# A two-layer kernel from its even output on: both token tiles through each step, or tile by tile with the row gathers of the tile ahead in between

## What is computed

```python
# l = 0: even mixer (convolution and pooling)       -> x   "e_out"
#        x = x + cross_attention(rmsnorm(x), mem)   -> "x_..."
#        x = x + peer_ffn(rmsnorm(x), ...)          -> "p_..."
# l = 1: x = x + sparse_attn_hgrn_mixer(rmsnorm(x)) -> "o_...", "h_...", the odd mixer
#        x = x + cross_attention(...)
#        x = x + peer_ffn(...)
# out = rmsnorm(x)

def peer_ffn(h, wq, sub_keys, u, v):              # per block of 128 tokens
    q = (xb @ wq).reshape(PEER_BLOCK, 8, 2, 128)
    s = jnp.einsum('thpd,hpnd->thpn', q, sub_keys)
    s1, i1 = lax.top_k(s[:, :, 0], 16)
    s2, i2 = lax.top_k(s[:, :, 1], 16)
    ...                                           # 16 x 16 sums, the best 16 of them per head
    g = jax.nn.softmax(top, axis=-1)              # 8 x 16 = 128 experts of 16384 for each token
    act = jax.nn.gelu(jnp.einsum('td,ted->te', xb, u[eid]))
    return jnp.einsum('te,ted->td', g * act, v[eid])
```

## Time and profile before

| | us |
|---|---|
| median of 3 runs | 2677.15 |
| profiled execution | 2676.58 |
| its span, first to last instruction | 2674.3 |
| last addition of the even output | 731 |
| gathers of layer 0, first issue | 885 |
| odd mixer, cross attention, queries of layer 1 | about 1580 to 2005 |
| last gather issued | 2641 |

### The profile page before, as it was taken

How to read it: one execution, slowest core, us unless ns; L and a number is a source line. 1 busy time by engine, 2 the same in 40 slices (tenths; PEclk the granted TensorE clock), 3 DMA queues, 4 the chain that set the end, 5 groups by cost and what they waited for, 6 DMA issues and landing times. The chain is left out here.

```text
span 2674.3 us, 23831 instructions
## 1 busy us (share of the span) xinstructions
PE 2111.0 (79%) x8566; PEld 1373.4 (51%) x8566; DVE 1453.6 (54%) x3135; ACT 653.1 (24%) x1247; POOL 1141.1 (43%) x809
## 2 busy tenths in 40 slices
PE   3899989999688498887778768858775887878776
PEld 3755679888577344333333337847672333333332
DVE  6353232147535977755555545672388776455554
ACT  1322333443233111111111124233331111111111
POOL 2612457797536333332333338214362333333332
PEclk7898989999898799999999989979898989989988
DMA  8455445565324599999999956113337999999996
GB/s 318 144 174 166 168 145 171 167 193 176 118 94 144 229 424 425 422 419 389 393 426 426 426 223 194 62 52 114 102 136 320 426 425 426 421 379 426 426 423 291
DMA packets 126934, 735.58 MB, mean 275 GB/s; under 512 B 14264, under 2 KB 14264, under 8 KB 60512
## 3 DMA queue, kind: packets, MB, share of 16 engines
q0 software_dynamic: 77600, 555.18, 49.9%
q1 hardware_dynamic: 49072, 178.83, 20.5%
q10 hardware_dynamic: 144, 0.05, 0.0%
HBM read 732.94 MB, written 1.06 MB: 274 GB/s over the span
## 5 line engine op out<-in xcount | busy, mean ns | idle before, releaser
L579 POOL TENSOR_TENSOR W_lo<-W,W_hi 128x1024 fp32r<-128x1024 f32 x264 | 642.6, 2442 | 423.7 <-ACT W_hi L1136 423.0
L800 PE MATMUL banks<-arena 128*128 128x512 f32 x912 | 449.5, 642 | 150.4 <-ACT arena L1191 150.4
L800 PE MATMUL banks<-rows_b,arena 128*128 128x512 f32 x684 | 341.1, 646 | 122.0 <-ACT arena L1191 122.0
L1136 ACT ACTIVATE W_hi<-W 128x1024 fp32r<-128x1024 f32 x264 | 277.4, 1058 | 471.3 <-PE banks L714 389.0
L800 PEld LDWEIGHTS banks<-arena 128*128 128x128 f32 x912 | 182.0, 204 | 405.3 <-issue 259.2
L2027 DVE SCALAR_TENSOR_TENSOR arena<-arena,banks 128x1024 f32<-128x1024 f32 x228 | 276.3, 1220 | 193.3 <-DMA arena<-in_uv,p_eid 192.1
L636 POOL DMA_INDIRECT arena<-in_uv,p_eid x228 | 214.8, 942 | 385.0 <-PE banks L800 376.4
L714 PE MATMUL banks<-HT_hi,W_hi 128*128 128x256 f32 x1128 | 327.2, 290 | 35.2 <-DVE HT_lo L1576 13.4
L714 PE MATMUL banks<-HT_hi,W_lo 128*128 128x256 f32 x1128 | 324.8, 288 | 0.0
L714 PE MATMUL banks<-HT_lo,W_hi 128*128 128x256 f32 x1128 | 324.6, 288 | 0.0
L800 PEld LDWEIGHTS banks<-rows_b,arena 128*128 128x128 f32 x684 | 138.7, 208 | 317.7 <-issue 206.9
(11 more groups left out here) (260 smaller groups left out, 2641.4 us busy)
## 6 DMA issues: line engine op xcount, KB each, us to landing
W<-in_weights SPq DMA_DIRECT2D x336, 512.0 KB, 3.6
gain<-in_rows POOLq DMA_DIRECT2D x10, 512.0 KB, 5.9
arena<-in_uv,p_eid POOLq DMA_INDIRECT x228
rows_b<-in_uv,p_eid POOLq DMA_INDIRECT x171
arena<-in_rows POOLq DMA_DIRECT2D x1, 2048.0 KB, 17.0
arena<-in_keys POOLq DMA_DIRECT2D x2, 1024.0 KB, 5.0
arena<-bias_scratch POOLq DMA_DIRECT2D x2, 1024.0 KB, 7.7
rows_c<-in_uv,p_eid POOLq DMA_INDIRECT x113, 10.9
```

The source lines that it names most:

```text
L579: po.tensor_tensor(W_lo[:, slot, :], W[:, (PARTS * n + part) % RAW_RING, :], W_hi[:, slot, :].bitcast(F32), ALU.subtract).then_inc(S_("lo_ ...
L800: mm = pe.matmul(sums[c], diag[:, n % DIAGS, :], rows[slot][:, D + c * BLK:D + (c + 1) * BLK], start=j == 0, stop=j == SEL - 1)
L1136: act.activation(W_hi[:, q % SPLIT_RING, :], wait_landed(act, n, part), ACT.Copy).then_inc(S_("hi_made"), 1)
```

## The change

The code up to the even output stays. From there on the work is cut into four chains, `CHAINS` = (layer 0, tile 0), (0, 1), (1, 0), (1, 1). Chain c does odd (layer 1), cross and query work of one token tile, and between its steps each engine has places (`feed`) at which it takes one group of rows of chain c-1. What is left of the groups after the chain runs at its end (`drain`); the rows of chain 3 come alone. In detail:

- Rows are taken in groups of two (64 groups a tile) instead of four, through a ring of eight slots instead of nine.
- At a feed DVE makes two dots and three small operations (L2098 to L2104 of the new file), ScalarE a tanh, two Identity with scale and bias, and two diagonals, PE the weighing of the group before. Gelu is written out with tanh.
- H of the gathers is read by DVE from SBUF; the two `p_h` banks go.
- Products are native fp32 (`dense`), tile by tile: 128 tokens moving under stationary weights, or 512 columns under stationary tokens, with a feed after each half of a weight tile. `high`, `low` and the splits of the activations go. Every weight tile of this part is read for both token tiles: 56 tiles instead of 30, counting those for the memory.
- GpSimd has only the gathers in its queue; keys, masks, gains and the bias table are loaded by SP in between the weights (`tables`), with waits of their own.
- Most copies out of PSUM move from DVE to ScalarE.
- The output is written tile by tile.

```diff
-RING = 9
-GROUP = 4
+RING = 8
+GROUP = 2
+CHAINS = [(l, t) for l in range(2) for t in range(2)]
...
+            def weigh(g):
+                c = at[0]
+                for j in range(g * GROUP, (g + 1) * GROUP):
+                    n, slot, turn = row_of(c, j)
+                    pe.wait_ge(S_("diag_ready"), n + 1)
+                    for b in range(2):
+                        mm = pe.matmul(banks[:, plan.bank(f"p_v{c}", b), :], diag[:, n % DIAGS, :],
+                                       rows[slot][:, D + b * BLK:D + (b + 1) * BLK], start=j == 0, stop=j == SEL - 1)
                     mm.then_inc(rows_done, 1)
...
+            def feed():
+                if at[0] is not None:
+                    if 1 <= at[1] <= GROUPS:
+                        weigh(at[1] - 1)
+                    at[1] += 1
...
+            def dense(stage, i, blocks):
+                n = tile_no[stage] + i
+                bank = claim(stage, i)
+                for part in range(PARTS):
+                    w = raw(n, part)
+                    for b, (out, columns, stationary) in enumerate(blocks):
+                        for j in range(2):
+                            x, y = w[:, j, columns], HT[:, 2 * part + j, :]
+                            mm = pe.matmul(bank[:, out], x if stationary else y, y if stationary else x,
+                                           start=part + b + j == 0,
+                                           stop=part == PARTS - 1 and b == len(blocks) - 1 and j == 1)
+                    mm.then_inc(pe_filled if part == PARTS - 1 else S_("part_used"), 1)
+                    if part % 2:
+                        feed()
...
+            def row_weights(g):
+                c = at[0]
+                e = slice(g * GROUP, (g + 1) * GROUP)
+                act.wait_ge(S_("dots_ready"), c * GROUPS + g + 1)
+                step(act.activation(p_tanh[:, e], p_poly[:, e], ACT.Tanh, scale=0.7978845608028654))
                 for j in range(g * GROUP, (g + 1) * GROUP):
+                    step(act.activation(p_w[:, j:j + 1], p_tanh[:, j:j + 1], ACT.Identity, scale=p_half[:, j:j + 1],
+                                        bias=p_half[:, j:j + 1]))
...
+                for n in range(PH // 2):
+                    feed()
+                    take(p_qT[l], f"p_q{n}.{c}")
+                    feed()
+                    if n:
+                        act.wait_ge(S_("lists_ready"), (PH // 2) * c + n)
+                    take(p_s[l], f"p_s{n}.{c}")
...
+                for n in range(PH // 2):
+                    after(v, f"p_s{n}.{c}")
+                    top_lists(l, n)
+                    if n < PH // 2 - 1:
+                        feed()
+                    candidates(l, 2 * n, 2 * n + 2)
+                    top_heads(l, 2 * n, 2 * n + 2)
+                    keys_of(l, t, 2 * n, 2 * n + 2)
+                    if n < PH // 2 - 1:
+                        feed()
+                if c == 1:
+                    feed(16)
...
             for c, (l, t) in enumerate(CHAINS):
+                if c:
+                    begin(c - 1)
+                if l:
+                    odd(c, t)
+                cross(c, l, t)
+                queries(c, l, t)
+                if c == 1:
+                    memory()
+                if c:
+                    drain()
+            begin(3)
+            drain()
```

More of the change, by code:

```diff
@@ L197, in make_plan @@
     p.add("e_out", 4)
[L198 to L246, removed]
+    for c, (l, t) in enumerate(CHAINS):
+        chain(p, c, l, t)
+        if c:
+            p.release(f"p_v{c - 1}")
+        p.add(f"p_v{c}", 2, marks=0, hold=True)
+    p.release("p_v3")
     return p
@@ L1017, in odd @@
-                for u in range(8):
-                    t, p = u // 4, u % 4
-                    bank = claim("idx", u)
+                after(pe, f"o_hq.{c}")
+                bank = claim(f"h_diag.{c}")
+                for hd in range(HH):
+                    mm = pe.matmul(bank[:, hd * P:(hd + 1) * P], h_kT[:, hd, :], h_qT[:, hd, :], start=True, stop=True)
+                mm.then_inc(pe_filled, 1)
+                dense(f"o_iq.{c}", 0, blocks4)
+                pe.wait_ge(S_("hscores_ready"), c - 1)
@@ L1194, in _, with take_turned, squares @@
+            def take_turned(stage):
+                for i in range(2):
+                    take(HT[:, 4 * i:4 * i + 4, :], stage, i)
+            def squares(t):
+                step(act.activation(H[:, t, :], X[:, t, :], ACT.Square, accum_out=stat(604, 1)), "squares_ready")
             act.dma_start(cols[:], io["cols"]).then_inc(S_("cols_in"), 16)
@@ L1399, in _ @@
[L1399 to L1400 removed]
+                step.free(act.activation(h_f, filled(act, f"o_hf.{c}"), ACT.Sigmoid), f"o_hf.{c}")
+                feed(2)
+                take(h_i[:, t, :], f"o_hi.{c}")
+                feed()
+                take(o_cT[:, t * P:(t + 1) * P], f"o_cT.{c}", cut=slice(0, P))
+                feed()
+                step(act.activation(h_g, filled(act, f"o_hg.{c}"), ACT.Sigmoid), "hg_sigmoid")
@@ new lines, in feed, with drain @@
+            def feed(n=1):
+                for _ in range(n):
+                    if at[0] is not None and at[1] < GROUPS:
+                        dots(at[1])
+                        at[1] += 1
+            def drain():
+                c = at[0]
+                l, t = CHAINS[c]
+                for g in range(at[1], GROUPS):
+                    dots(g)
+                at[0] = None
+                v.wait_ge(rows_done, (c + 1) * SEL)
+                for b in range(2):
+                    xs = X[:, t, b * BLK:(b + 1) * BLK]
+                    step.free(v.tensor_tensor(xs, banks[:, plan.bank(f"p_v{c}", b), :], xs, ALU.add), f"p_v{c}", b)
```

1244 lines of the change are left out of this document (702 added, 542 removed).

## The result

The changed kernel takes **2555.4 us** (median of 4 runs, 2553.9 to 2559.3), the one before 2680.7 in the same series. The ratio is **0.9535**, 95% interval 0.9511 to 0.9558. The forecast said 2627 us, 1.9% less than before; the gain is 125 us where 50 were forecast. Because the kernel before moved a little from series to series (medians of 2680.7 to 2686.6 us), small differences between two changed kernels are given by medians and, where it matters, by the two ratios to before as well. The profiled execution has a span of 2557.4 us.

What follows compares the result with a forecast made beforehand. Gathers were taken as DMA-bound, the work between them not, so the change overlaps the two. 731 + 150 + 448 + 483 + 495 + 318 = 2625 us of span, predicted as 2627; 8-in-10 range 2450 to 2760.

Steps and rivals of the forecast that it cites:

- What bounds the kernel, and which stretches would change: Row gathers are bound by DMA, the 154 + 425 us between them are not; everything to 731 us stays.
- the price of a list pass: Query work: one DVE pass of four score blocks and two heads takes 17.6 us, the first 21.3.
- Half a tile with a group, 7.2: Weight products with row weighing: PE takes (3.4 + 3.4)/0.95 = 7.2 us at a granted clock of 0.95.
- A level: Odd work, chains 2 and 3: four DVE operations of 0.69 and a group, 5.9 us each, 47 for eight.
- the odd parts' 28: Odd work of chains 2 and 3, forecast at 538 us together and measured at 510.
- That TensorE sets the dense slot: Half tiles with a group: PE sets the 7.2 us, although DMA needs 7.4, as parts and rows are there beforehand.
- The ring: Eight row slots turn in 19.7 us; the median landing of 10.9 fits, the worst, 16.1, would add 90.
- ScalarE's 2.1 us: Query list passes: DVE waits three times 2.1 us a chain while ScalarE copies scores behind the group's 1.4.
- The last rows: Chain 3's rows alone: 6 for the norm, 60 groups x 4.92 = 295, and 17 from last landing, 318 us.
- elastic: Rival, chance 0.18: rings and prefetch smooth the slots, each stage costs only its largest total, DMA; 2381 us.
- Low clock: Rival, chance 0.17: waits between PE's pieces lower the clock to 0.72, PE-bound slots cost 9.5; +193, 2820 us.
- Serial slots: Rival, chance 0.13: in 63 slots without weight tile engines wait for each other, 9.3 instead of 5.3; +252, 2879.

Runs made afterwards that it cites:

- half the products: Changed kernel leaving out every second product of the weight tiles in chains 1 to 3, loads unchanged: 2540.5 us, ratio 0.9455.
- half the bytes: Changed kernel leaving out half the bytes of each weight part in chains 1 to 3, products unchanged: 2541.6 us, ratio 0.9476.
- the experiment: Changed kernel with six row slots instead of eight, nothing else: 2675.1 us, ratio 0.9948.

## Right and wrong, by the prediction's steps

- **What bounds the kernel, and which stretches would change**: right. DMA share 9 lies in the dense parts, stages came in the forecast order, gathers began at 817 (forecast 826) and ended at 2528 (2590).
- **The step that failed** is the price of a list pass, read in the earlier trace rows from the first two passes, 21.3 and 17.6 long, and carried over unchanged to all 16. Measured: 14.3. 16 times 3.3, and 3.7 for the first, are 56 of the 68 us: the 17 of chain 0 and the 39 of the queries. Two things stood in those rows that the change removes. GpSimd was making low halves, which cost 2.6 us a pass and 3.7 more in the first: about 45 of the 56. And VectorE copied the scores itself, 0.7 us a pass: about 12. The prediction removed GpSimd's low halves as work off the path and did not ask whose time they had been taking; and it counted ScalarE's copy as a wait without taking VectorE's out. The trace of before had both answers: its fourth pass takes 15.0 us, and the median of L1998 over its 32 runs was 0.68 us, its longest 2.9. The Trainium skill states the rule (SBUF — State Buffer, section SBUF: two separate sides): one port pair is shared, and whichever of GpSimd and a VectorE operation with two SBUF inputs, or in a two-port mode, starts first keeps it for its whole instruction. The runs agree as to which operations get longer; that the shared port is the reason is the Trainium skill's word, and no run here looks at ports. The Trainium skill gives no price for a pass; its rule says which rows to distrust, and the price stood in the trace of before.
- **Half a tile with a group, 7.2**: measured 6.86 to 7.01. The clock's 0.95 was the mis-sized factor, 9 to 15 us over the 44 half tiles of both odd parts. A level took 5.65 (forecast 5.9), 4 us for all 16, and chain 3's larger key count cost 3 us, not 12: with these most of the odd parts' 28 is told. In the cross parts the shorter slots gained nothing. They ran at a DMA share of 1.02 in chains 2 and 3, and chain 2's took 98.3 us, 98.4 with half the products, 95.6 with half the bytes and 88.5 with both.
- **That TensorE sets the dense slot**: half right. Bytes and products have to fall together. Its result was near, because the two limits lie within a few per cent.
- **The ring**: the median was the right choice; the experiment gives 17.2 us for the loop of six slots.
- **ScalarE's 2.1 us**: right, 2.44 measured, and it could be taken out.
- **The last rows**: 17 too few. The forecast had 6 us ahead of them. GpSimd's timeline at their start (start, duration, idle before):

```profile
2212.21 0.98 POOL L713 DMA_INDIRECT rows_c<-in_uv,p_eid  x1 [1.49 <-PE banks L845]
2237.50 0.94 POOL L713 DMA_INDIRECT arena<-in_uv,p_eid  x1 [24.31 <-PE banks L845]
```

Nothing is gathered for 24 us: a slot comes free only behind additions (2222.5), norm, dots, row weights and weighing, 15 us where I had counted 6. From that gather to the landing of the last row (2541.0) it is 303.5 us and not 60 x 4.92 = 295. The likely reason, which no run tests, is the first row's own way from issue to landing, which nothing hides. The 16.4 us from there to the end were forecast at 17. VectorE's last dot with a wait:

```profile
2541.00 1.22 DVE L2097 SCALAR_TENSOR_TENSOR rows_c<-rows_c,H 128x1024 f32<-128x1024 f32 x1 [1.16 <-DMA rows_c<-in_uv,p_eid]
```
- **Rivals**: *elastic* gave 2381; its mechanism, the transfers, was one of the two limits, but in the list stretches the DMA share fell to 0.72 to 0.90, as was said against it. *Low clock*: 0.94 to 1.00 where groups and products alternate; chain 0 shows 0.80 and the query stretches 0.84 to 0.92, where TensorE waits for VectorE anyway. The rule of a stream cut by waits (the Trainium skill, TensorE: Matmul & The Clock Gate, section HAM oscillation) agrees with the rows there; the dense stretches, where TensorE's waits were at most 2.5 us but for the norm, kept the high clock. *Serial slots*: the levels at 5.65 exclude it.

The middle value was 72 us too high: 68 are in the table, and the rest is that the profiled execution was the slowest of the four.

## What to carry over

Before a duration is carried into a forecast, look at what ran on the neighbouring engine in that row, and at which of the row's own operations the change moves away; the shortest instance of the same stretch elsewhere in the trace is the price without a neighbour. Where two resources stand at full use side by side, test them together: each alone moved 14 to 21 us here, both 72 to 76. And an engine that stands idle in a stretch with a fixed length is the place for work that has no one to hide it, as long as the copies behind it don't stand ahead of something that the path needs.

## What was not expected of the hardware

A GpSimd elementwise operation from SBUF to SBUF holds up some VectorE operations and not others: in the kernel before, p_eid took 2.27 us instead of 0.19 and a pair of 128x512 products 3.48 instead of 1.3, with the busy time booked on VectorE, not as idle time; the max and find-index operations beside them kept their durations of 0.07 to 0.87 us. The gathers that GpSimd issues did next to nothing of the kind: the pass with eight of them in it took 14.4 us. And the ring turned out to have about 2.5 us to spare in a turn of 19.7; two slots fewer cost 120 us.
